# Banded attention: inverses of the softmax sums spread by products and applied to the outputs of four steps

## The reference

```python
s_band = jnp.where(valid, q @ k_band.T, NEG)        # 3 blocks of keys, 2 at the edges
s_ctx = q @ k_ctx.T                                 # 256 keys
p = softmax(concatenate([s_band, s_ctx, s_sink]))   # the sink takes part in the sum only
o = p_band @ v_band + p_ctx @ v_ctx
```

## Time and profile before

| | us |
|---|---|
| median of 3 runs | 2565.39 (2563.78 to 2566.22) |
| span of the profiled execution | 2565.7 |
| busy in it: PE, PEld, DVE, ACT, POOL | 2381.1, 1817.7, 1225.6, 860.2, 33.5 |
| attention: first scores to the next stage's first product | 1063.20 to 1195.59 |

### The profile page before, as it was taken

One profiled execution on the slowest core, in us unless ns is written; L12 is line 12 of the kernel. 1 busy time (PEld: TensorE's weight loads), 2 busy tenths in 40 slices (PEclk: granted clock), 3 DMA queues, 4 the chain that ended last, 5 costly groups with the idle time before them and its releaser, 6 DMA issues. The chain is left out here.

```text
span 2565.7 us, 33772 instructions
## 1 busy us (share of the span) xinstructions
PE 2381.1 (93%) x13722; PEld 1817.7 (71%) x13722; DVE 1225.6 (48%) x1918; ACT 860.2 (34%) x1318; POOL 33.5 (1%) x57
## 2 busy tenths in 40 slices
PE   6998889999999979799899999997999979999997
PEld 4983779999999976577688888874797743333322
DVE  3698445552455342475564465655554332222224
ACT  5115553331233242385443244345454321100101
POOL 0000000000000001100000000000000000000000
PEclk8999989999999989899899999999999989999998
DMA  5256311121112125101223233210241469999996
GB/s 239 73 158 248 124 42 66 60 85 44 66 57 82 59 100 227 63 2 42 83 95 110 82 101 102 85 62 1 80 151 34 173 260 421 421 421 421 421 421 260
DMA packets 74242, 387.51 MB, mean 151 GB/s; under 512 B 8576, under 2 KB 12928, under 8 KB 43264
## 3 DMA queue, kind: packets, MB, share of 16 engines
q1 hardware_dynamic: 74112, 385.66, 39.7%
HBM read 380.22 MB, written 2.10 MB: 149 GB/s over the span
## 5 line engine op out<-in xcount | busy, mean ns | idle before, releaser
L264 DVE TENSOR_TENSOR WLO<-RAW,WHI 128x1024 fp32r<-128x1024 f32 (+3 forms) x226 | 279.2, 1236 | 703.9 <-ACT WHI L253 703.3
L309 PE MATMUL PS<-XNH,WHI 128*128 128x384 f32 (+2 forms) x1888 | 593.5, 358 | 15.5 <-DVE WLO L264 4.7
L309 PE MATMUL PS<-XNH,WLO 128*128 128x384 f32 (+2 forms) x1888 | 585.5, 354 | 0.0
L309 PE MATMUL PS<-XNL,WHI 128*128 128x384 f32 (+2 forms) x1888 | 585.1, 354 | 0.0
L253 ACT ACTIVATE WHI<-RAW 128x1024 fp32r<-128x1024 f32 (+3 forms) x226 | 241.4, 1068 | 803.6 <-PE PS L309 784.4
L309 PEld LDWEIGHTS PS<-XNH,WHI 128*128 128x128 f32 x1888 | 349.2, 189 | 53.9 <-issue 14.7
L309 PEld LDWEIGHTS PS<-XNL,WHI 128*128 128x128 f32 x1888 | 349.5, 189 | 30.9 <-issue 2.4
L309 PEld LDWEIGHTS PS<-XNH,WLO 128*128 128x128 f32 x1888 | 349.2, 189 | 29.9
L2780 PE MATMUL PS<-RAWM,XS 128*64 128x512 f32 x1016 | 238.2, 600 | 16.7 <-DMA RAWM<-experts 15.9
L2780 PEld LDWEIGHTS PS<-RAWM,XS 128*64 128x64 f32 x1016 | 66.3, 136 | 152.9 <-issue 92.1
L309 PE MATMUL PS<-HH,WHI 128*128 128x384 f32 (+1 forms) x528 | 157.9, 353 | 0.0
(11 more groups left out here) (357 smaller groups left out, 2592.9 us busy)
## 6 DMA issues: line engine op xcount, KB each, us to landing
RAWM<-experts SPq DMA_DIRECT2D x191, 1024.0 KB, 17.0
RAW<-up SPq DMA_DIRECT2D x88, 512.0 KB, 3.2
ADAW<-ada SPq DMA_DIRECT2D x40, 1024.0 KB, 7.9
RAW<-down SPq DMA_DIRECT2D x32, 704.0 KB, 4.1
RAW<-pw SPq DMA_DIRECT2D x24, 512.0 KB, 3.5
ADAL<-ada SPq DMA_DIRECT2D x8, 1024.0 KB, 6.4
RAW<-qkv SPq DMA_DIRECT2D x12, 512.0 KB, 3.3
RAW<-w_in SPq DMA_DIRECT2D x10, 512.0 KB, 3.4
```

Source lines behind the costliest of these rows:

```text
L264: dve.tensor_tensor(prog.WLO[:, at % SPLITS, 0:to.length], prog.RAW[:, at % RAWS, 0:to.length], f32(prog.WHI[:, at % SPLITS, 0:to.length]) ...
L309: last = pe.matmul(prog.PS[:, to, at:at + b - a], w, x[:, k, a:b], start=(k == 0 and n == 0), stop=(k == g.k - 1 and n == 2))
```

## The change

The probabilities stay unnormalised. VectorE takes the reciprocals of both sums of a step in one instruction (`invert`) and keeps those of four steps in `factor`. TensorE gets a new piece of work after scores(n+3) and before values(n) of every b3: `spread_factors`, eight products whose weight is a column of `factor` repeated 64 times and whose moving operand is the identity, so that every row of a head's 64 output rows gets the factors of the four blocks along its 512 columns. It takes a place of its own in the turn of the two transpose banks. ScalarE copies that bank to `WIDE` (`keep_factors`), right after the copies of b3. VectorE then multiplies the output bank by `WIDE` into `SCALED` (`scale_out`), and `XNH` (`keep_hi`, now after the exponentials that follow b0's copies) and `XNL` (`keep_lo`) are made from `SCALED`. transposes(n) waits for the exponentials of n in place of the products. The output bank comes free with scale_out.

```diff
--- before.py
+++ after.py
@@ -1392,13 +1392,16 @@
         BUFS, AT = 3, 8
         T = reg.take("T", [P, BUFS, 2, AT + 5 * BLOCK])
         PT = reg.take("PT", [P, 2, 5, 2, BLOCK])
-        stats = reg.take("STATS", [P, BUFS, 2, 4])
+        least_of, total = reg.take("LEAST", [P, BUFS, 2]), reg.take("TOTAL", [P, BUFS, 2])
+        factor = reg.take("FACTOR", [P, 2, NB, 2])
+        WIDE, SCALED = reg.take("WIDE", [P, LAT]), reg.take("OUTS", [P, LAT])
         nsink = reg.take("NSINK", [P, HEADS])
         PS = prog.PS
         negated, sunk, scored, maxed = prog.sem("negated"), prog.sem("sunk"), prog.sem("scored"), prog.sem("maxed")
-        exped, inverted, normed = prog.sem("exped"), prog.sem("inverted"), prog.sem("normed")
+        exped, inverted = prog.sem("exped"), prog.sem("inverted")
+        spread, wide_kept, out_scaled = prog.sem("spread"), prog.sem("wide_kept"), prog.sem("out_scaled")
         turned, copied, attended = prog.sem("turned"), prog.sem("copied"), prog.sem("attended")
-        out_hi, out_free = prog.sem("out_hi"), prog.sem("out_free")
+        out_hi, out_lo = prog.sem("out_hi"), prog.sem("out_lo")
         halves = (slice(0, 64), slice(64, 128))
 
         def keys(b):
@@ -1416,9 +1419,21 @@
 
             return [range(c, min(c + 2, len(chunks(n)))) for c in range(0, len(chunks(n)), 2)]
 
-        first_group = [0]
+        first_group, items = [], 0
         for n in range(STEPS):
-            first_group.append(first_group[-1] + len(groups(n)))
+            first_group.append(items)
+            items += len(groups(n)) + (n % NB == NB - 1)
+
+        def factors_at(t):
+
+            return first_group[NB * t + NB - 1] + len(groups(NB - 1))
+
+        def copies_before(at):
+
+            return at - sum(factors_at(t) < at for t in range(STEPS // NB))
+
+        def bank(at):
+            return PS[:, 2, at % 2 * 512:at % 2 * 512 + 512]
 
         def out(n):
             return PS[:, 3, n // NB % 2 * 512:n // NB % 2 * 512 + LAT]
@@ -1448,25 +1463,41 @@
                                      prog.KT[rows, t // 4, kb[0] * BLOCK:(kb[-1] + 1) * BLOCK], start=True, stop=True)
                 last.then_inc(scored, 1)
 
+            def bank_free(at):
+
+                if at >= 2 and at - 2 in [factors_at(t) for t in range(STEPS // NB)]:
+                    pe.wait_ge(wide_kept, [factors_at(t) for t in range(STEPS // NB)].index(at - 2) + 1)
+                elif at >= 2:
+                    pe.wait_ge(copied, copies_before(at - 2) + 1)
+
             def transposes(n):
-                pe.wait_ge(normed, 2 * n + 2)
+                pe.wait_ge(exped, 2 * n + 2)
                 for g, group in enumerate(groups(n)):
                     at = first_group[n] + g
-                    if at >= 2:
-                        pe.wait_ge(copied, at - 1)
+                    bank_free(at)
                     for c in group:
                         for h in range(2):
-                            to = at % 2 * 512 + (2 * (c - group[0]) + h) * P
-                            last = pe.transpose(PS[:, 2, to:to + P], T[:, n % BUFS, h, AT + c * P:AT + (c + 1) * P],
+                            to = (2 * (c - group[0]) + h) * P
+                            last = pe.transpose(bank(at)[:, to:to + P], T[:, n % BUFS, h, AT + c * P:AT + (c + 1) * P],
                                                 prog.IDENT[:])
                     last.then_inc(turned, 1)
+
+            def spread_factors(t):
+
+                pe.wait_ge(inverted, NB * t + NB)
+                bank_free(factors_at(t))
+                for b in range(NB):
+                    for h in range(2):
+                        last = pe.matmul(bank(factors_at(t))[64 * h:64 * h + 64, b * BLOCK:(b + 1) * BLOCK],
+                                         factor[:, t % 2, b, h:h + 1].to_broadcast([P, 64]), prog.IDENT[:], start=True, stop=True)
+                last.then_inc(spread, 1)
 
             def values(n):
                 t, b = n // NB, n % NB
                 if b == 0 and t >= 2:
-                    pe.wait_ge(out_free, t - 1)
+                    pe.wait_ge(out_scaled, t - 1)
                 for g, group in enumerate(groups(n)):
-                    pe.wait_ge(copied, first_group[n] + g + 1)
+                    pe.wait_ge(copied, copies_before(first_group[n] + g) + 1)
                     for c in group:
                         for h, rows in enumerate(halves):
                             head = (2 * (t // 4) + h) * HEAD_DIM
@@ -1482,6 +1513,8 @@
                 transposes(n)
                 if n + BUFS < STEPS:
                     scores(n + BUFS)
+                if n % NB == NB - 1:
+                    spread_factors(n // NB)
                 values(n)
 
         @block.vector
@@ -1492,38 +1525,47 @@
             def maxima(n):
 
                 dve.wait_ge(scored, n + 1)
+                if n >= BUFS:
+                    dve.wait_ge(inverted, n - BUFS + 1)
                 mask = prog.MASKS[:, 0 if n % NB == 0 else 1, 0:width(n)]
                 for h in range(2):
                     head = 2 * (n // NB) + h
                     dve.tensor_tensor_reduce(T[:, n % BUFS, h, AT:AT + width(n)], PS[:, h, CTX:CTX + width(n)], mask,
                                              1.0, nsink[:, head:head + 1], ALU.add, ALU.min,
-                                             stats[:, n % BUFS, h, 0:1]).then_inc(maxed, 1)
-
-            def normalise(n):
-                for h in range(2):
-                    dve.wait_ge(exped, 2 * n + h + 1)
-                    dve.reciprocal(stats[:, n % BUFS, h, 2:3], stats[:, n % BUFS, h, 1:2]).then_inc(inverted, 1)
-                for h in range(2):
-                    p = T[:, n % BUFS, h, AT:AT + width(n)]
-                    dve.wait_ge(inverted, 2 * n + h + 1)
-                    dve.tensor_scalar(p, p, stats[:, n % BUFS, h, 2:3], None, ALU.mult).then_inc(normed, 1)
+                                             least_of[:, n % BUFS, h:h + 1]).then_inc(maxed, 1)
+
+            def invert(n):
+                dve.wait_ge(exped, 2 * n + 2)
+                t, b = n // NB, n % NB
+                dve.reciprocal(factor[:, t % 2, b, :], total[:, n % BUFS, :]).then_inc(inverted, 1)
+
+            def scale_out(t):
+
+                dve.wait_ge(attended, t + 1)
+                dve.wait_ge(wide_kept, t + 1)
+                if t >= 1:
+                    dve.wait_ge(out_lo, t)
+                dve.tensor_tensor(SCALED[:], out(NB * t), WIDE[:], ALU.mult).then_inc(out_scaled, 1)
 
             def keep_lo(t):
 
                 dve.wait_ge(out_hi, t + 1)
-                dve.tensor_tensor(prog.XNL[:, t, 0:LAT], out(NB * t), f32(prog.XNH[:, t, 0:LAT]),
-                                  ALU.subtract).then_inc(out_free, 1)
+                dve.tensor_tensor(prog.XNL[:, t, 0:LAT], SCALED[:], f32(prog.XNH[:, t, 0:LAT]),
+                                  ALU.subtract).then_inc(out_lo, 1)
 
             for n in range(BUFS):
                 maxima(n)
-            normalise(0)
+            invert(0)
             for n in range(STEPS):
+                if n % NB == 0 and n > 0:
+                    scale_out(n // NB - 1)
                 if n + 1 < STEPS:
-                    normalise(n + 1)
+                    invert(n + 1)
                 if n + BUFS < STEPS:
                     maxima(n + BUFS)
                 if n % NB == 0 and n > 0:
                     keep_lo(n // NB - 1)
+            scale_out(STEPS // NB - 1)
             keep_lo(STEPS // NB - 1)
 
         @block.scalar
@@ -1533,25 +1575,37 @@
                 for h in range(2):
                     p = T[:, n % BUFS, h, AT - 1:AT + width(n)]
                     act.wait_ge(maxed, 2 * n + h + 1)
-                    act.activation(p, p, ACT.Exp, bias=stats[:, n % BUFS, h, 0:1], scale=-1.0,
-                                   accum_out=stats[:, n % BUFS, h, 1:2]).then_inc(exped, 1)
+                    act.activation(p, p, ACT.Exp, bias=least_of[:, n % BUFS, h:h + 1], scale=-1.0,
+                                   accum_out=total[:, n % BUFS, h:h + 1]).then_inc(exped, 1)
 
             def copies(n):
                 for g, group in enumerate(groups(n)):
                     at = first_group[n] + g
-                    act.wait_ge(turned, at + 1)
+                    act.wait_ge(turned, copies_before(at) + 1)
                     act.activation(PT[:, n % 2, group[0]:group[-1] + 1, :, :].rearrange("p c h q -> p (c h q)"),
-                                   PS[:, 2, at % 2 * 512:at % 2 * 512 + 2 * P * len(group)], ACT.Copy).then_inc(copied, 1)
+                                   bank(at)[:, 0:2 * P * len(group)], ACT.Copy).then_inc(copied, 1)
+
+            def keep_factors(t):
+                act.wait_ge(spread, t + 1)
+                if t >= 1:
+                    act.wait_ge(out_scaled, t)
+                act.activation(WIDE[:], bank(factors_at(t)), ACT.Copy).then_inc(wide_kept, 1)
+
+            def keep_hi(t):
```

(10 more changed lines are left out.)

## The result

| | before | changed |
|---|---|---|
| median of the runs, us | 2564.6 (6 runs) | 2574.2 (6 runs) |
| ratio to before | | 1.0035 (1.0024 to 1.0045) |
| span of the profiled execution | 2565.7 | 2573.6 |
| attention, first scores to next stage's first product | 132.39 | 139.98 |
| first transposes after the stage's first scores | 13.33 | 10.47 |

What follows compares the result with a forecast made beforehand. The prediction took TensorE's program order to bound the kernel's attention stage, with VectorE's products covered. Its terms +7.0 + 7.1 + 0.7 - 2.8 = +12.0 us gave 2577.4 us, range 2569.0 to 2584.5.

Steps and rivals of the forecast that it cites:

- b3: Attention step on the last of four query blocks (4 chunks of keys); 3.33 us long before the change.
- spread, eight times: TensorE, once per pair of heads before the values: 0.87 us each, all on the path, +7.0 us.
- new wait in b1, seven times: TensorE's last two transposes wait for ScalarE's copy, queued behind the factors' copy: 1.0 us each, +7.1 us.
- b1: Attention step on the second of four query blocks, with 5 chunks of keys.
- scale_out at the end: End of the attention stage: values, scale_out, high and low parts stand in a row, +0.7 us.
- first transposes' wait: Start of the stage: transposes no longer wait for VectorE's first product, -2.8 us.
- clock's earlier rise: TensorE's clock at the stage's start: no extra gain taken; ends of the start's gain 1.3 and 2.8 us.
- ScalarE's detour is hidden: Rival: ScalarE's idle time takes up the wait for the spread, sum +4.9 us, 2570.3 us; chance 0.15.
- unpaired spread: Rival: the spread's column halves don't run side by side on TensorE, 8 x 0.87 us more, 2584.4 us; chance 0.10.
- faster: Rival: VectorE's product traffic lengthens TensorE's and ScalarE's hand-overs; removal saves up to 20.3 us, 2557.1 us; chance 0.04.
- The clock didn't fall for the stalls: Rival judged: stalls bring TensorE's low clock back, some 1.4 us in 7 pairs of heads, 2587.2 us; chance 0.05.
- The walk: ScalarE's queue followed from the factors' copy to TensorE's last two b1 transposes: 9.67 us against 8.65 unhindered.

Runs made afterwards that it cites:

- e2: The changed kernel with the eight products of each spread done twice into the same columns; 2579.3 us, ratio to before 1.0057.
- e1: The changed kernel with ScalarE's copy of the factors moved behind the exponentials of n+2; 2567.4 us, ratio to before 1.0009.
- e9: The changed kernel with the first transposes again waiting for two VectorE products, here into a scratch tile; 2577.9 us, ratio to before 1.0058.
- e3: The kernel before without its 64 VectorE products, so without normalisation, transposes waiting for the exponentials; 2560.4 us, ratio to before 0.9985.
- e4: The changed kernel with 64 VectorE products of the same size put back, writing an unread scratch tile; 2573.2 us, ratio to before 1.0033.

## Why the prediction was right, and where it was off

The forecast was 2577.4 us, 12.0 us more; measured were 9.0, and 7.59 in the stage itself. By its own terms:

| term | forecast | measured in the stage | from |
|---|---|---|---|
| spread, eight times | +7.0 | +7.0 | b3 4.20 for 3.33; e2 |
| new wait in b1, seven times | +7.1 | +4.6 | 0.90 for 0.25; e1 gave back 4.58 |
| scale_out at the end | +0.7 | +0.8 | 6.17 - 4.48 less one spread of 0.87 |
| first transposes' wait | -2.8 | -2.9 | 13.33 to 10.47; e9, e3 |
| clock's earlier rise | 0 | -1.9 | 4.72 less 2.86; e9 gave 1.4 |
| sum | +12.0 | +7.6 | |

Of the 0.8 at the end, 0.70 lie between the values and the next stage's product (3.84 us for 3.14), and the last spread waits 0.34 for its bank where the values waited 0.25. For the clock at the end the forecast took 0; outside attention the two profiles differ by 0.3 us.

**Right**: that TensorE bounds the stage, so that VectorE's products buy nothing in the steady part (e3 and e4); that the spread costs all its length and pairs its halves (e2); that ScalarE's program order makes a new wait at b1's last transposes (e1); that scale_out adds its length once, at the end. The rival "ScalarE's detour is hidden" is refuted by the trace, "unpaired spread" by 0.87, and "faster" by e3's period. The clock didn't fall for the stalls either: over 110 us of the steady part it is 1.00 in the changed kernel, so a wait of 0.90 in each pair of heads did not bring the low level back.

```profile
1084.00:1194.00 110.00, 102.66 (x1062) 77.04 (x1062) 54.24 (x150) 81.41 (x189) 4.70 (x25) 1.00 0.01 2
```

**Off by size, the wait in b1**: 1.0 forecast, 0.65 measured. The walk took 1.77 us for a pair of exponentials, from 1136.37 to 1138.14. What started at 1138.14 was the copy of the output, and that waits for values which by the earlier trace rows end at 1137.00 + 1.09 = 1138.09. So 0.14 of the 1.77 was a wait, read as work. In the changed kernel the pair takes 1.63 (1124.50 to 1126.13, and again 1127.09 to 1128.71), twice in the walk, and keep_hi 0.52 and not 0.58. With these three the walk ends 0.34 earlier, at 9.33, and the wait comes to 0.68. A row shows idle time in brackets only from some size on; a step of the chain has to be measured where the next instruction had nothing to wait for.

**Off by a term, the clock at the start**: the text put its end at 2.8 us of gain, "since the work in front of the rise is the same". It is not: the gap of 2.8 us was part of what stood in front of the rise, and with it gone the clock rose some 7 us earlier. (e9 gave back 1.4 of the 1.9 because its clock rose at 18.3 us and not at 19.3 as in the kernel before.) This bound should have been open on the side of the gain. The first error made the change look 2.5 us worse, the second hid 1.9 us that closing this gap brings. Both lie on the same side, so neither covered up the other.

## What to carry to other kernels

Work that is taken from an engine which waits for another was worth nothing here, though it was a third of that engine's busy time; look for the one place where the bounding engine waits for it, and try to move the work there before paying for its removal with instructions on the bounding engine (here 5 us for a new order of a few lines). When a new wait enters an in-order engine, walk everything queued behind it until the next hand-over to the bounding engine: here a copy placed one line later was worth 4.6 us. And take the durations of such a walk from rows whose successor was not itself waiting.

## What the runs showed of the hardware

- A weight read with a stride of zero loaded and streamed like any other: a load of 64 columns took 136 ns for the spread and for the values, 16 more records of the spread cost 0.87 us (e2), and 4 more records of values 0.21.
- A float32 transpose is one record of 0.107 us for 128 columns, a float32 product of the same columns two, so a broadcast along the rows done as a transpose streams in half the time; 0.15 us of that goes back at the change of phase.
- A gap of 2.8 us in TensorE's work at the low clock level delayed the rise to the high one by about 7 us (11.6 to 12.6 us after the first scores without it, 18.3 to 19.6 with it). Closing it was worth 4.7 us and not 2.9.
